# Paged sparse attention of eight sample sequences: from whole-page gathers with a penalty mask to half-page loads and gathers of selected rows

## The chip, the cores and the metric

One core of a Trainium2 chip runs the whole program. The metric is the device time of one execution in microseconds; lower is better. The engines are TensorE (PE, with its weight loads as PEld), VectorE (DVE), ScalarE (ACT), GpSimd (POOL) and SyncE (SP), and 16 DMA engines move data.

## The reference, cut to what matters

The program is one step of a two-layer decoder trunk for a prompt of 512 tokens and for eight sample sequences of one token each. The part that changes is the attention of the sample tokens, once per layer. Each sequence has 4096 past tokens in a paged cache: 32 pages of 128 tokens, four vectors a token (k_cmp, v_cmp, k_sel, v_sel), for 2 groups of 64 numbers. One token is 2 KB, and its first 1 KB is k_cmp and v_cmp.

```python
ck = compress_blocks(k_cmp, ...)      # blocks of 32 tokens, stride 16: 255 rows
cv = compress_blocks(v_cmp, ...)
p_c = masked_softmax(q @ ck * scale + head_bias(rel_bias, dist_c), dist_c >= 0)
o_c = p_c @ cv
p_s = sum over the 4 heads of a group of p_c @ overlap       # a score for each 64-token block
score = where(forced, SEL_FORCE, p_s)                        # first block and the last two are forced
_, idx = top_k(score, 16)                                    # for each sequence and group
o_s = softmax(q @ k_sel[idx] * scale + bias) @ v_sel[idx]
o_w = softmax(q @ k_win * scale + bias) @ v_win              # 512 window tokens and the new one
o = g0 * o_c + g1 * o_s + g2 * o_w
```

## The kernel before, in words

The program is a row of stages, each a block at whose end all engines meet. In each layer the sample attention is one such stage, between the prompt attention and the stage that computes the channel gates (L1695 on). Nothing of the other stages runs beside it, except that SP has loaded the first weights of the next stage ahead. The loop over tiles: a sequence is 8 tiles of 512 tokens. `gather` (L1271 to L1277) copies a column of row numbers into `cell` and issues one indirect DMA on POOL: each of 128 partitions gets 4 whole tokens, 8 KB, 1 MB in all. So all four vectors of all 4096 tokens come in.

For each tile TensorE does this in `turn` and `use`: 8 transposes of k_cmp and v_cmp (L1321), 4 of k_sel (L1326), 4 matmuls with the first compression weights `w1` (L1337), and 4 matmuls of k_sel with the queries `q_blk`, 8 columns each (L1345). DVE lays k_cmp and v_cmp apart (L1497) and copies v_cmp transposes out of PSUM (L1510), ACT those of k_cmp (L1444) and of k_sel (L1448), POOL keeps v_sel (L1285).

The rest of a sequence is `chain`, cut into 13 slots that are put between the tiles of the next sequence by `in_turn`. It has keys in partitions and the 8 heads in columns: second compression matmul, compressed scores, softmax (a maximum over partitions takes a transpose, a reduction and a matmul with `ones`), block scores, top 16 by max and match_replace, a penalty of -1e30 spread to all unselected keys by a small matmul with `rt`, softmax of all 4096 selected-branch scores and the window's, and at slot 11 the value matmuls: 32 over `v_sel` (L1421), 4 over the window (L1424) and a few small ones. For the last sequence the chain runs with nothing beside it.

The setup stage (from time 0) makes the tables: `key_bias` by 40 small matmuls (L695), row numbers from 16 small page-table DMAs on POOL (L628), the input transposes (L716) and the prompt's bias table by a DRAM round trip and 8 `flip` matmuls (L724).

Of the kernel before, what the change touches and what calls it, by code (L numbers as in the profile page):

```python
# [57 lines left out]
BLK = 38  # L58
NEWS, WIN0, NEWW = 32, 33, 37
# [16 lines left out]
def shape_constants():  # L76
# [5 lines left out]
    dist = np.zeros((BLK, P), np.int64)  # L82
    for b in range(32):
        dist[b] = PAST - (STRIDE * (P * (b // 16) + p) + b % 16)
    for t in range(4):
        dist[WIN0 + t] = WINDOW - 4 * p - t
    cmp_dist = np.stack([PAST - (STRIDE * (P * t + p) + CMPB - 1) for t in range(2)])
    keys = onehot(np.concatenate([dist, cmp_dist]))
# [4 lines left out]
    rt = (s[:, None] == n // 4).astype(np.float32)  # L93
    new = np.where(np.arange(NB)[:, None] == np.arange(NB), 0.0, NEG).astype(np.float32)
    kmask = np.zeros((P, 40), np.float32)
    kmask[0, WIN0] = NEG
    kmask[P - 1, 39] = NEG
    chunk = (p % 8).astype(np.float32).reshape(P, 1)
    return {"line": line, "keys": keys.reshape(NBUCK, 40 * P), "ov": ov.reshape(2, P, SELB + 1).transpose(1, 0, 2).copy(),
            "rt": rt, "new": new, "chunk": chunk, "kmask": kmask, "ident": np.eye(P, dtype=np.float32),  # L100
            "flip": np.ascontiguousarray(np.eye(P, dtype=np.float32)[::-1])}
# [19 lines left out]
def build(nc, A, O):  # L121
# [26 lines left out]
    used = {}  # L148

    def sb(scope, name, shape, dt=F32):  # L150

        used[name] = used.get(name, 0) + 1
        if used[name] > 1:
            name = f"{name}_{used[name]}"
        return scope.enter_context(nc.sbuf_tensor(name, shape, dt))

    with stack:
# [12 lines left out]
        rt = sb(stack, "rt", [SELB + 1, 2 * P])  # L170
        key_bias = sb(stack, "key_bias", [P, 40, N_HEADS])
        new_bias = sb(stack, "new_bias", [NB, NB, N_HEADS])
        gather_rows = sb(stack, "gather_rows", [P, NB * 8], U32)
# [366 lines left out]
        cvs = at("cvs", [P, 2, P], F32, offset=w_hi_at + KC * P * 4)  # L540
# [3 lines left out]
        def layer_buffers(L):  # L544
# [4 lines left out]
            for where, name, shape in (("b4", "oac", [P, 6, TOK]), ("b4", "u_c", [P, 2, CC - 1 + TOK]), ("b4", "us_c", [P, 2, CC, NB]),  # L549
                                       ("b3", "w1", [P, 2, 8, P]), ("b3", "w2", [P, 2, P]), ("b3", "b2row", [P, P]), ("b3", "cbias", [P, 2]),  # L550
                                       ("b3", "gateT", [NG_W, TOK]), ("b3", "k_new", [P, 2, NB]), ("b3", "nat_new", [NB, KV_W]),
                                       ("b3", "q_blk", [P, NB, N_HEADS]), ("b2", "z", [P, 20, TOK])):
                S[name] = sb(S[where], f"{name}{L}", shape)
# [8 lines left out]
        with phase_semaphores(), ExitStack() as scope:  # L562
# [6 lines left out]
            keys = sb(scope, "keys", [NBUCK, 40 * P])  # L569
# [176 lines left out]
        for L in range(DEPTH):  # L746
          with phase_semaphores():
# [442 lines left out]
            with phase_semaphores(), ExitStack() as scope:  # L1190
# [62 lines left out]
                def restart_chain(e):  # L1253
                    if e is nc.vector:
                        dve_chain.restart(e)
# [977 lines left out]
```

## Time and profile before

| | |
|---|---|
| Median of 3 runs | 3768.5 us (3766.31 to 3784.81) |
| The profiled execution | 3775.46 us, its span 3773.6 us |
| PE, PEld, DVE, ACT, POOL busy | 89%, 84%, 39%, 25%, 9% |
| Mean granted TensorE clock | 0.856 of 2.4 GHz |
| Moved by DMA | 347.87 MB, mean 92 GB/s |

The span runs from the first to the last instruction; the time of an execution adds 1.9 us around it. Busy shares are averages over stages with different limits. Matmuls in plain f32 appear as two records each and transposes as one, so a count of 64 records at L1421 is 32 matmuls.

### The profile page before, as it was taken

How to read it: one execution, taken by the hardware profiler on the slowest of the kernel's cores; microseconds unless marked ns; L12 is line 12 of the kernel's file. 1: busy time of each engine (PE TensorE's matmuls, PEld its weight loads, DVE VectorE, ACT ScalarE, POOL GpSimd, SP SyncE). 2: the span in 40 equal slices, each digit the busy share in tenths (PEclk: the TensorE clock that was granted, in tenths of full speed). 3: DMA queues.
4: the chain of work that ended last, by engine and by line, in shares of the span. 5: the costliest groups of instructions: out<-in, count | busy, mean ns of one | idle time of the engine just before them, and what ended most of it. 6: DMA issues, size and time to landing. Idle time of an engine off the chain costs nothing. (4 is left out here: it accounts for less than half of the span.)

```text
span 3773.6 us, 57697 instructions
## 1 busy us (share of the span) xinstructions
PE 3364.6 (89%) x22978; PEld 3161.3 (84%) x22978; DVE 1478.1 (39%) x3319; ACT 953.1 (25%) x1827; POOL 351.9 (9%) x470
## 2 busy tenths in 40 slices
PE   5979799898899878999999797989879996899998
PEld 4966688888799868999989566888879996889997
DVE  2235533333646322433231554333427533143322
ACT  0223322221123312222222333221212332132221
POOL 1000122221000100000010002222200000010000
PEclk8977888887799866999989679888969997689998
DMA  5320244342233311233232204443413323023331
GB/s 142 90 81 15 79 164 162 134 150 73 68 85 95 102 60 40 77 92 88 87 80 57 79 12 170 145 154 130 162 28 88 89 82 123 10 65 95 90 89 58
DMA packets 353413, 347.87 MB, mean 92 GB/s; under 512 B 36001, under 2 KB 323110, under 8 KB 336238
## 3 DMA queue, kind: packets, MB, share of 16 engines
q1 hardware_dynamic: 334238, 210.34, 18.8%
q0 software_dynamic: 18944, 134.24, 10.3%
q8 instruction: 170, 2.79, 0.3%
q14 instruction: 61, 0.50, 0.0%
HBM read 333.85 MB, written 19.55 MB: 94 GB/s over the span
## 5 line engine op out<-in xcount | busy, mean ns | idle before, releaser
L313 PE MATMUL pg<-act_hi,w_lo 128*128 128x260 f32 x3072 | 633.9, 288 | 42.7 <-PEq L140 12.6
L285 DVE TENSOR_TENSOR w_lo<-w_raw,w_hi 128x1024 fp32r<-128x1024 f32 x296 | 370.5, 1252 | 712.7 <-ACT w_hi L278 711.7
L313 PE MATMUL pg<-act_hi,w_hi 128*128 128x260 f32 x3072 | 628.0, 287 | 0.0
L313 PE MATMUL pg<-act_lo,w_hi 128*128 128x260 f32 x3072 | 627.4, 286 | 0.0
L313 PEld LDWEIGHTS pg<-act_hi,w_lo 128*128 128x128 f32 x3072 | 484.4, 193 | 47.6 <-issue 32.7
L313 PEld LDWEIGHTS pg<-act_hi,w_hi 128*128 128x128 f32 x3072 | 482.9, 192 | 0.0
L313 PEld LDWEIGHTS pg<-act_lo,w_hi 128*128 128x128 f32 x3072 | 482.8, 192 | 0.0
L278 ACT CAST w_hi<-w_raw 128x1024 fp32r<-128x1024 f32 x296 | 308.5, 1042 | 281.0 <-PE pg L313 141.7
L1448 ACT COPY w_raw<-pg 128x512 f32<-128x512 f32 x144 | 84.6, 587 | 442.1 <-PE pn L1345 439.8
L1421 PE MATMUL pn<-pr,v_sel 128*128 128x8 f32 x1024 | 184.6, 324 | 0.0
L1421 PEld LDWEIGHTS pn<-pr,v_sel 128*128 128x128 f32 x1024 | 183.6, 284 | 0.0
L1321 PE MATMUL pg<-ident,apart 128*128 128x128 f32 x1024 | 161.0, 308 | 14.0 <-DVE apart L1497 14.0
L352 POOL TENSOR_TENSOR norm_r<-norm_ms,minus_half 128x5 f32<-128x5 f32 x12 | 14.1, 1173 | 1609.5 <-DVE norm_ms L348 1609.5
L1321 PEld LDWEIGHTS pg<-ident,apart 128*128 128x128 f32 x1024 | 133.4, 163 | 18.1 <-issue 14.9
L1274 POOL COPY cell<-gather_rows 128x1 uint32 (+1 forms) x128 | 28.4, 222 | 1252.1 <-POOLq L140 691.5
L313 PE MATMUL pg<-hid_hi,w_lo 128*128 128x260 f32 x704 | 142.9, 284 | 0.0
L313 PE MATMUL pg<-hid_hi,w_hi 128*128 128x260 f32 x704 | 141.5, 282 | 0.0
L313 PE MATMUL pg<-hid_lo,w_hi 128*128 128x260 f32 x704 | 141.4, 282 | 0.0
L1345 PEld LDWEIGHTS pn<-q_blk,w_raw 128*128 128x128 f32 x1024 | 134.4, 192 | 6.7
L1276 POOL DMA_INDIRECT cache<-in_cache_kv,cell x128 | 129.9, 1015 | 71.3 <-POOL cell L1274 69.0
L1337 PE MATMUL pg<-xkv,w 128*128 128x256 f32 x512 | 132.3, 404 | 0.0
L1337 PE MATMUL pg<-w_raw,w 128*128 128x256 f32 x512 | 128.7, 396 | 0.9 <-issue 0.2
(407 smaller groups left out, 5504.3 us busy)
## 6 DMA issues: line engine op xcount, KB each, us to landing
w_raw<-in_w_ffn_in SPq DMA_DIRECT2D x88, 512.0 KB, 3.8
w_raw<-in_w_in SPq DMA_DIRECT2D x80, 512.0 KB, 3.8
cmem<-in_cache_mem SPq DMA_DIRECT2D x16, 1024.0 KB, 13.4
w_raw<-in_w_ffn_out SPq DMA_DIRECT2D x32, 512.0 KB, 4.1
win<-in_cache_win SPq DMA_DIRECT2D x16, 512.0 KB, 3.5
w_raw<-in_w_o SPq DMA_DIRECT2D x16, 512.0 KB, 4.2
w_raw<-in_w_xkv SPq DMA_DIRECT2D x16, 512.0 KB, 4.2
out_win_sample<-in_cache_win SPq DMA_DIRECT2D x2, 4088.0 KB
```

Source lines behind the costliest of these rows:

```text
L278: e.copy(w_hi[:, v % 2, :], w_raw[:, v % RING, :]).then_inc(whi_ready, 1)
L285: e.tensor_tensor(w_lo[:, v % 2, :], w_raw[:, v % RING, :], w_hi[:, v % 2, :].bitcast(F32), ALU.subtract).then_inc(w_ready, 1)
L313: mm = e.matmul(pg[:, ts, h, 0:wd], w[:, v % 2, wk], x[:, k0 + k, at:at + wd], start=first and k == 0 and n == 0, stop=last and k == kn - ...
L352: e.tensor_tensor(self.r[:], self.ms[:], minus_half[:, 0:5], ALU.pow).then_inc(rstd_ready, 1)
L1274: e.tensor_copy(cell[:, k % 4:k % 4 + 1], gather_rows[:, bass.ds(b * TILES + k, 1)]).then_inc(cell_set, 1)
L1276: e.indirect_dma_start(out=cache[:, k % 4, :], out_offset=None, in_=rows_dram, in_offset=bass.IndirectOffsetOnAxis(ap=cell[:, k % 4:k % 4 ...
L1321: mm = e.transpose(pg[:, 0, kv, at:at + P], apart[:, k % 2, 2 * kv + g, 2 * pair:2 * pair + 2, :].rearrange("p t d -> p (t d)"), ident[:])
L1337: e.matmul(pg[:, 1, 1, kv * 256:(kv + 1) * 256], w1[:, kv, 2 * (k % 4) + pair, :], xkv[k % 2][:, kv, pair * 256:(pair + 1) * 256], start=k ...
L1345: mm = e.matmul(pn[:, 0, (4 * k + t) * 8:(4 * k + t + 1) * 8], k_sel[:, t * P:(t + 1) * P], q_of(b), start=True, stop=True)
L1421: e.matmul(pn[:, 1, 8:16], v_sel[:, par, t, :], pr[:, t, :], start=t == 0, stop=False)
L1448: e.copy(k_sel[:], pg[:, 1, 0, :]).then_inc(ks_ready, 1)
```

## The change

The sample attention stage is rewritten; the setup makes other tables for it.

- **Half pages.** SP loads for each page only the k_cmp and v_cmp half: 128 tokens of 1 KB, into 8 partitions of `ring`. The page number is read from SBUF into a register (`value_load`) before each of these DMAs. 16 pages make a group of 2 MB; there are 16 groups a layer, so 256 loads and 256 DMAs. `ring` holds two groups.
- **First phase.** POOL lays each half group apart (32 copies of 128x2048). PE makes 136 steps: 128 of 4 transposes and, two steps later, 2 matmuls with `w1`; then 8 for the windows, of 4 transposes and one matmul against the queries. Between them stand the second compression and the compressed scores of each sequence.
- **One chain for all sequences.** The queries sit in `qpad`, 64 columns of which 8 belong to a sequence, so that scores of all eight gather in one PSUM tile with 64 rows (8 sequences by 8 heads) and keys in columns. Softmax is along a row: a maximum from one `tensor_tensor_reduce`, an exponential that also sums. Block lists come from `max` and `max_index`; 13 picked blocks and the forced ones become row numbers `gidx`.
- **Second phase.** POOL issues 16 indirect DMAs for a sequence (8 parts by 2 groups), each of 128 rows of 1 KB (k_sel and v_sel), 128 a layer, all after `gidx` is there. `sel` holds four sequences. PE then transposes the keys, scores them, and after the softmax of a pair of sequences (`q`) multiplies the values.
- Loops over sequences are written out; before they were loops with registers.
- In the setup, 40 small matmuls and the 16 page-table DMAs are gone; two matmuls of 64 rows make `rowbias`, two DMAs on SP bring the page table.

```diff
--- before.py
+++ after.py
@@ setup: tables
-                    for a in range(16):
-                        e.dma_start(pages[8 * a:8 * a + 8, :, :],
-                                    A["page_table"].rearrange("b (t a) -> a b t", a=16)[a:a + 1].broadcast_to([8, NB, 2]), allow_slow_non_contiguous=True
-                                    ).then_inc(ldp, 16)
-                    e.wait_ge(ldp, 256)
+                    for g in range(2):
+                        e.dma_start(pages[g * NB:(g + 1) * NB, :], A["page_table"]).then_inc(ld, 16)
...
+                    for h in range(2):
+                        mm = e.matmul(pg[0:64, 0, h, 0:512 if h == 0 else RB_END - 512], rel8[:].rearrange("p b h -> p (b h)"),
+                                      rows_oh[:, h * 512:512 if h == 0 else RB_END], start=True, stop=True)
@@ sample attention: SP
+                        for n in range(NT):
+                            if n >= 2:
+                                e.wait_ge(laid, 2 * n - 2)
+                            for a in range(16):
+                                page = e.value_load(page_row[0:1, 16 * n + a:16 * n + a + 1])
+                                e.dma_start(ring[8 * a:8 * a + 8, n % 2, :, :],
+                                            A["cache_kv"][L:L + 1, bass.ds(page, 1), :, 0:2].rearrange("l o (c q) k g d -> (l o c) q (k g d)", q=16)
+                                            ).then_inc(got[n % 2], 16)
@@ POOL
+                        for j in range(2 * NT):
+                            n, kv = j // 2, j % 2
+                            if kv == 0:
+                                e.wait_ge(got[n % 2], 256 * (n // 2 + 1))
+                            if j >= 2:
+                                e.wait_ge(turned, 4 * (j - 1))
+                            e.tensor_copy(apart[:, kv].rearrange("p g t d -> p t g d"),
+                                          ring[:, n % 2, :, kv * P:(kv + 1) * P].rearrange("p t (g d) -> p t g d", g=2)).then_inc(laid, 1)
+                        e.wait_ge(gidx_s, 1)
+                        for b in range(NB):
+                            if b == 1:
+                                e.wait_ge(sc_s, NB)
+                            elif 2 <= b < 4:
+                                e.wait_ge(ocw_s, 1)
+                            elif b >= 4:
+                                e.wait_ge(q_pv, (b - 4) // 2 + 1)
+                            for t in range(8):
+                                for g in range(2):
+                                    e.indirect_dma_start(out=sel[:, place[b % 4], t, g, :], out_offset=None, in_=rows_kv,
+                                                         in_offset=bass.IndirectOffsetOnAxis(ap=gidx[:, t, g * NB + b:g * NB + b + 1], axis=0)
+                                                         ).then_inc(sel_in[b], 16)
@@ PE
+                        for m in range(WSTEPS + 4):
+                            if m < WSTEPS:
+                                turn(m)
+                            if 2 <= m < WSTEPS + 2:
+                                use(m - 2)
+                            if (b := at_step(m, 23)) is not None:
+                                compressed(b)
+                            if (b := at_step(m, 27)) is not None:
+                                score_c(b)
...
+                        for b in range(NB):
+                            for hh in range(2):
+                                ktile(b, hh)
+                                kscore(b, hh)
+                            if b % 2:
+                                pturn(b // 2)
+                                values(b // 2)
@@ DVE
+                        link(e.max(top[:, 0:8], score[:]))
+                        link(e.max_index(idx[:, 0:8], top[:, 0:8], score[:]))
+                        link(e.match_replace(score[:], top[:, 0:8], score[:], -1.0))
+                        link(e.max(top[:, 8:16], score[:]))
+                        link(e.max_index(idx[:, 8:16], top[:, 8:16], score[:]))
```

The first place is SP, at the start of the sample attention of the first layer. Before, it issues two window loads and then a loop (L1265) of two more a trip, each with its address computed in a register (ISA) and each a 128x1024 DMA:

```order
L1262 DMA win<-in_cache_win 128x1024 x2
L1265 UNCONDITIONAL_BRANCH
L1265 ISA
L1262 ISA
L1262 DMA win<-in_cache_win 128x1024
L1262 ISA
L1262 DMA win<-in_cache_win 128x1024
L1265 REGISTER_ALU
L1265 COMPARE_AND_BRANCH
```

Now the same place has the page table's load and then three rows for each page, the load of a register, an address computation and a DMA of 8 partitions:

```order
L1267 DMA page_row<-in_page_table 1x256
L1273 TENSOR_LOAD page_row [waits pages_in]
L1274 ISA
L1274 DMA ring_3887<-in_cache_kv 8x16x256
L1273 TENSOR_LOAD page_row
L1274 ISA
L1274 DMA ring_3887<-in_cache_kv 8x16x256
```

The pair of rows repeats 256 times a layer; SP had 272 rows in the whole program and has 1800.

The second place is POOL in the same stage. Before, a gather of 8 KB rows stands between copies, and each waits for its tile buffer:

```order
L1285 COPY v_sel<-cache 128x512 [waits got0]
L1274 COPY cell<-gather_rows 128x1 [waits v_kept,tr_s]
L1276 DMA cache<-in_cache_kv,cell 128x2048 [waits cell_set]
L1285 COPY v_sel<-cache 128x512 [waits got1]
L1274 COPY cell<-gather_rows 128x1 [waits v_kept,tr_s]
L1276 DMA cache<-in_cache_kv,cell 128x2048 [waits cell_set]
```

Now POOL's 32 copies come first (the last two are shown), and all gathers follow them, with a wait at the head of each sequence's 16:

```order
L1290 COPY apart_3889<-ring_3887 128x16x2x64 [waits turned,got1]
L1290 COPY apart_3889<-ring_3887 128x16x2x64 [waits turned]
L1302 DMA sel<-in_cache_kv,gidx 128x256 [waits gidx_s]
L1302 DMA sel<-in_cache_kv,gidx 128x256 x15
L1302 DMA sel<-in_cache_kv,gidx 128x256 [waits sc_s]
L1302 DMA sel<-in_cache_kv,gidx 128x256 x15
L1302 DMA sel<-in_cache_kv,gidx 128x256 [waits ocw_s]
L1302 DMA sel<-in_cache_kv,gidx 128x256 x15
```

The gathers moved from beside the tiles to behind all of them. The third place is PE. Before, one tile of 512 tokens is this:

```order
L1321 MATMUL pg<-ident,apart 128x128 [waits xk_ready,staged]
L1321 MATMUL pg<-ident,apart 128x128 x3
L1321 MATMUL pg<-ident,apart 128x128 [waits xv_ready]
L1321 MATMUL pg<-ident,apart 128x128 x3
L1326 MATMUL pg<-ident,cache 128x128 [waits ks_ready]
L1326 MATMUL pg<-ident,cache 128x128 x3
L1337 MATMUL pg<-w_raw,w 128x256 [waits xk_ready]
L1337 MATMUL pg<-w_raw,w 128x256
L1337 MATMUL pg<-w_raw,w 128x256 [waits xv_ready]
L1337 MATMUL pg<-w_raw,w 128x256
L1345 MATMUL pn<-q_blk,w_raw 128x8 [waits ks_ready]
L1345 MATMUL pn<-q_blk,w_raw 128x8 x3
```

Now 512 tokens are two steps, of these rows, and the second compression (L1349, L1351) stands between steps once in 16:

```order
L1318 MATMUL pg<-ident,apart_3889 128x128 [waits laid,ev0]
L1318 MATMUL pg<-ident,apart_3889 128x128 x3
L1334 MATMUL pg<-w_raw,w 128x256 [waits ev0]
L1334 MATMUL pg<-w_raw,w 128x256
L1318 MATMUL pg<-ident,apart_3889 128x128 [waits ev1]
L1318 MATMUL pg<-ident,apart_3889 128x128 x3
L1334 MATMUL pg<-w_raw,w 128x256 [waits ev1]
L1334 MATMUL pg<-w_raw,w 128x256
```

The transposes and score matmuls of k_sel left the tile.

## Rows read from the trace of the kernel before

**Rows 1.** The page: the span and the engines' busy time and shares.

```profile
span 3773.6 us, 57697 instructions
PE 3364.6 (89%) x22978; PEld 3161.3 (84%) x22978; DVE 1478.1 (39%) x3319; ACT 953.1 (25%) x1827; POOL 351.9 (9%) x470
```

**Rows 2.** Windows: both attention stages, then parts of the first; busy us, PEclk, DMA share, GB/s.

```profile
450.00:976.00 526.00, 461.43 (x2794) 428.10 (x2794) 188.37 (x549) 104.10 (x200) 122.67 (x192) 0.81 0.40 136
2298.00:2813.00 515.00, 449.65 (x2794) 417.83 (x2794) 188.20 (x549) 104.13 (x200) 121.51 (x192) 0.83 0.40 139
...
466.00:490.00 24.00, 23.88 (x170) 22.13 (x170) 9.08 (x13) 7.29 (x14) 12.39 (x19) 1.00 0.88 299
...
540.00:546.00 6.00, 6.00 (x28) 5.90 (x28) 0.27 (x2) 0.00 (x0) 0.00 (x0) 0.50 0.00 0
```

**Rows 3.** Timeline, start and us: first and last instructions of the two stages.

```profile
450.24 0.82 SPq L1262 DMA_DIRECT2D win<-in_cache_win  x2
...
974.83 0.35 DVE L1603 COPY oac<-o 64x4 f32<-64x4 f32 x2
...
2298.27 0.19 POOL L1274 COPY cell<-gather_rows 128x1 uint32<-128x1 uint32 x1 [347.62 <-POOLq L140]
...
2811.70 0.35 DVE L1603 COPY oac<-o 64x4 f32<-64x4 f32 x2
```

**Rows 4.** Timeline of PE in one tile, and the value matmuls of two sequences.

```profile
467.07 1.07 PE L1321 MATMUL pg<-ident,apart 128*128 128x128 f32 x8
468.44 1.89 PE L1337 MATMUL pg<-xkv,w 128*128 128x256 f32 x8
470.17 0.95 PE L1345 MATMUL pn<-q_blk,w_raw 128*128 128x8 f32 x8
...
530.58 12.16 PE L1421 MATMUL pn<-pr,v_sel 128*128 128x8 f32 x64
...
957.64 13.80 PE L1421 MATMUL pn<-pr,v_sel 128*128 128x8 f32 x64
```

**Rows 5.** SP and POOL: durations ns min/median/max of DMA issues and register work; landing.

```profile
L1262 SPq DMA_DIRECT2D win<-in_cache_win x16: 332/336/427, 450.2 to 2699.4; - x16
L1262 SPq FUSED_REGOPS  x12: 43/46/66, 545.7 to 2699.3; - x12
...
L1276 POOL DMA_INDIRECT cache<-in_cache_kv,cell x128: 958/961/1536, 451.1 to 2730.7; - x128
...
L1285 POOL COPY v_sel<-cache x128: 610/627/1132, 458.9 to 2736.2; 128x512 f32<-128x512 f32 x128
...
w_raw<-in_w_c_out SPq DMA_DIRECT2D x16, 128.0 KB, 2.4
```

**Rows 6.** DMA queues: packets, MB, share of the 16 engines over the span.

```profile
q1 hardware_dynamic: 334238, 210.34, 18.8%
q0 software_dynamic: 18944, 134.24, 10.3%
```

**Rows 7.** Timeline of the setup: PE, SP, and the first weight conversion of the next stage.

```profile
24.10 17.23 PE L695 MATMUL pg<-rel,keys 32*128 32x8 f32 x80
...
33.97 0.37 SPq L618 DMA_DIRECT2D toep_up<-line_scratch  x1
...
42.95 5.33 PE L716 MATMUL pa<-ident,x_nat 128*128 128x128 f32 x24
...
53.54 7.61 PE L724 MATMUL pg<-toep_up,flip 128*128 128x512 f32 x16
...
73.99 1.04 ACT L278 CAST w_hi<-w_raw 128x1024 fp32r<-128x1024 f32 x1 [55.16 <-PEq L140]
```

**Rows 8.** DMA issues: KB, and median us to landing of the bias line's load.

```profile
toep_up<-line_scratch SPq DMA_DIRECT2D x1, 2048.0 KB, 7.8
```

**Rows 9.** Timeline of the prompt attention: DVE and ACT on rows of 512.

```profile
2268.29 0.69 DVE L1094 CUSTOM_DVE_ANT_0 s_lg<-pg,toep_h 128x512 f32<-128x512 f32 x1
...
2269.34 0.72 ACT L1160 ACTIVATE s_lg<-s_lg,nmx 128x512 f32<-128x512 f32 x1
```

More of the change, by code:

```diff
@@ L80, in shape_constants @@
     line = onehot(np.maximum(SEQ - 1 - m, 0))
[L82 to L88, printed above, removed]
+    slot = np.arange(SELB)
+    w = np.arange(WINDOW)
+    far = onehot(np.full(SELB, PAST))
+    rows = np.concatenate([
+        onehot(PAST - (STRIDE * np.arange(2 * P) + CMPB - 1)), onehot(WINDOW - (4 * (w % P) + w // P)), onehot(np.zeros(1, np.int64)),
+        np.zeros((NBUCK, SELB), np.float32), onehot(SELB - slot) - far, onehot(np.zeros(1, np.int64)) - far[:, 0:1],
+        onehot(2 * SELB - slot) - far], axis=1)
     n = np.arange(2 * P)
@@ L1467, in _ @@
-                        in_turn(e, tiles, chain)
+                        for m in range(WSTEPS + 4):
+                            if m < WSTEPS and m % 2 == 0:
+                                e.wait_ge(turned, m + 1)
+                                if m >= 4:
+                                    e.wait_ge(used, m - 3)
+                                e.copy(stag[m % 4], pg[:, 0, 0, :]).then_inc(ev[0], 1)
+                            for t in range(2):
+                                if (b := at_step(m, 9 + 8 * t)) is not None:
+                                    keep_half(e, 2 * b + t, c_act, 1)
+                            if (b := at_step(m, 20)) is not None:
+                                e.wait_ge(pre_s, b + 1)
+                                e.activation(second[:, :, 0:2 * P], first[:], ACT.Tanh, scale=0.5).then_inc(th_s, 1)
+                            if (b := at_step(m, 25)) is not None:
+                                e.wait_ge(cmp_s, b + 1)
+                                if b >= 2:
+                                    e.wait_ge(sc_s, b - 1)
+                                e.activation(ck[:, b % 2, :], pn[:, 0, 0:256], ACT.Identity, bias=vecs[:, V_B2:V_B2 + 1]).then_inc(ck_s, 1)
@@ L1605, in _ @@
[L1605 to L1609 removed]
+                            if (b := at_step(m, 25)) is not None:
+                                e.wait_ge(cmp_s, b + 1)
+                                e.tensor_tensor(cv[:, b], pn[:, 1, 0:256].rearrange("p (t x) -> p t x", t=2),
+                                                b2row[:].rearrange("p (o x) -> p o x", o=1).broadcast_to([P, 2, P]), ALU.add).then_inc(cv_s, 1)
```

798 lines of the change are left out of this document (393 added, 405 removed).

## The prediction

> **What bounds the kernel now.** I read the page first [rows 1]. PE is busy 89% of the span, which says little about one stage, so I went on to the windows [rows 2]. The sample attention takes 450.24 to 975.18 in the first layer, 524.9 us, and 2298.27 to 2812.05 in the second, 513.8 us [rows 3]: together 1038.7 us, 28% of the span. In it PE is busy 461 of 526 us at a granted clock of 0.81, while DVE has 188, ACT 104 and POOL 123, and DMA is at 40% [rows 2]. So PE bounds the stage, and the reader should see that its clock is not one value: 1.00 among the tiles (466 to 490) and 0.50 in the value matmuls (540 to 546). The timeline gives the prices at full clock: 1.07 us for the 8 transposes of k_cmp and v_cmp in a tile, 1.89 us for its 4 matmuls with `w1`, 0.95 us for its 4 matmuls of k_sel with the queries [rows 4]. The 32 value matmuls of a sequence cost 12.16 us, or 0.38 us each, at the low clock [rows 4]. Beside the last sequence nothing runs, and its value matmuls take 13.80 us with everyone waiting [rows 4].
>
> **What leaves PE.** A sequence loses 32 transposes of k_sel, the 32 small score matmuls over all keys and most of the value matmuls. What a tile keeps, 1.07 + 1.89 us, is now two steps of 1.48 us. I add 1.6 us a sequence for the second compression and its scores (four matmuls, priced from the 0.47 us of one with 256 columns, 1.89 / 4). A window step has 4 transposes (0.54), one matmul of 512 columns (7.61 / 8 = 0.95, [rows 7]) and a small one: 1.7 us. PE's work in the first phase is 8 x (16 x 1.48 + 1.6) + 8 x 1.7 = 216 us, or 12.6 us for a group of 16 pages. That alone would end the stage early. The question is who feeds it.
>
> **First phase: SP.** SP now does three things for each of 256 pages: a register load, an address computation, a DMA. Two of them have rows: an address computation 0.046 us, a DMA with a computed address 0.336 us [rows 5]. The register load has none. Bounds: not below the 0.05 us of a register operation, not above the 2.4 us that the quickest DMA in the page takes from issue to landing [rows 5], since that contains a read of memory and much besides. I am nearer to neither row, so I reason from the second: it holds descriptor making, a read, a write and a semaphore, and the register load is the read alone, a quarter to a third. I take 0.7 us. A page then costs s = 0.70 + 0.05 + 0.34 = 1.09 us, a group 17.4 us against PE's 12.6. **SP becomes the bound of the phase.** Length: page table there 2.9, 256 x 1.09 = 279, last landing 2.4, POOL's copy 2.5 (4 x 0.627, [rows 5]), the last 8 steps 11.8, windows 13.6, last compression 1.6: **314 us**. POOL's 32 copies (5 us a group) and the copies of DVE and ACT lie beside that. The ring of two groups does not bind: a slot comes free about when SP has issued the group before.
>
> The Trainium skill, "DMA: Bandwidth & Descriptors", Latency and other measured facts, gives about 600 ns as the floor of a tensor_load. By it the phase would be 288 us and the kernel 3633 us; no row here shows it.
>
> **The transfers.** The queues give 34 ns for a packet on one engine at a mean of 629 bytes (0.188 x 16 x 3773.6 / 334238) and 328 ns at 7086 bytes [rows 6]; a straight line puts a row of 1 KB at 52 ns. A group has 2048 rows: 6.7 us over 16 engines, hidden under 17.4. A DMA into 8 partitions may not use all of them; over 8 engines it is 13.3 us, still hidden, but it would bind if the register load cost under 0.44 us. The same page of the Trainium skill, How many engines (k), says that the largest number up to 16 that divides the slowest dimension of both sides is used, here 8. By it the floor of my range for a free register load is 3552 us, by 16 engines 3518.
>
> **Between the phases.** Until the first gather may go there is one serial chain with nothing beside it: about 25 small DVE operations at 0.2 to 0.25 us, three over 806 numbers (1.35 ns each from 0.69 us for 512, [rows 9]) 3.3 us, two exponentials and row reads 1.5 us, 16 matmuls that spread the row numbers at 0.38 us, six handovers. Sum **18 us**, no less than 12 and no more than 28.
>
> **Second phase: POOL.** 128 gathers of 128 rows. An indirect issue takes POOL 0.961 us and has 128 rows before as well [rows 5], so 123 us, all after the last score, where before they lay beside PE. Then the last sequence: landing 2.4; transposes, scores, copies 4.6; softmax over 961 numbers 4.7 (1.3 and 1.35 for the two long ones after [rows 9]); turning and keeping 1.8; the 36 value matmuls of a pair at 0.38, 13.7; the last addition 0.6. Together **151 us**. The gathers of the fifth sequence wait until the first pair's values are done: landed at 33 us, done at about 58, and POOL comes there at 61. Slack of 3 us, so no stall in the sum.
>
> **Setup.** The 40 matmuls of L695 hold PE for 17.23 us, and the input transposes and flips follow [rows 7]. With them gone the flips wait for the load of the bias line instead, issued at 33.97 and landed 7.8 us later [rows 7, 8]. They start at 41.8, not 53.54, and each later event, the weight conversion at 73.99 included, moves up by **11.7 us**.
>
> **Sum.** Stage 314 + 18 + 151 = 483 us; 41.9 and 30.8 us less than the two of before, with the setup 84 us less. Against this execution's 3775.46 us that is 3691; the median of the runs shown is 7 us lower, so 3684. With s free the time is 3684 + 512 x (s - 1.09): each 0.1 us of a page's issue is 51 us, and **at s = 1.25, a register load of 0.87 us, the gain is gone**. Half a percent, 19 us, is about what a measurement can tell from no change.
>
> **Rivals.**
> - *The register load costs 0.9 us or more* (slower). Place: SP at L1273. At 1.1 us s is 1.49, each first phase 102 us longer, time 3889. For: the load lies in the path of every page, nothing overlaps it on SP, and no row bounds it well. Against: only my split of the 2.4 us. Chance 0.33. At the far bound of 2.4 us it would be 4555.
> - *SP is fast and PE or the transfers bind.* Register load below 0.6 us; 3518 to 3635, by the work of 216 us or the 8 engines. For: register operations are cheap in all rows. Chance 0.14.
> - *The second phase costs more.* An issue of 1.3 us (the longest row is 1.54) gives 43 us a layer, a missed slack at the fifth and seventh sequence 5 us each. Time 3740 to 3790: no change that can be told. Chance 0.10.
> - *PE's clock stays low.* With gaps of 5 us a group PE might run at 0.50 as in 540 to 546: a step of 2.96, a group of 25 us, time about 3970. Against: at half clock PE would have no gaps, and among dense tiles it is granted 1.00. Chance 0.05.
> - *The forecast*: s from 1.0 to 1.19, 3640 to 3735 us. Chance 0.38.
>
> **Numbers.** Faster 0.38 + 0.14 = 0.52, same 0.10, slower 0.33 + 0.05 = 0.38. The cases have both signs, so the range must reach into them: 3600 to 3980 leaves out a register load under 0.54 us and one above 1.28 us, some 0.2 together.
>
> **What would show it.** The register load's duration on SP; the distance between page DMAs, 1.09 us; POOL's laying copies waiting for DMA and not for PE; first phase of 314 us; 128 gathers back to back at 0.96 us, PE mostly idle under them; L278 first at about 62 us. I am wrong if POOL waits for PE in the first phase, or if SP's row is far from 0.7.

## The result, and the profile after

The changed kernel takes **4105.8 us** (median of 4 runs, 4093.9 to 4115.6) against 3768.3 us before (4 runs): ratio 1.088, 95% interval 1.084 to 1.093. It is slower by 9%; the forecast was 3685 us. The profiled execution took 4115.6 us.

The page of the changed kernel, beside [rows 1]:

```profile
span 4113.8 us, 52582 instructions
PE 3158.6 (77%) x20942; PEld 2874.3 (70%) x20942; DVE 1335.2 (32%) x2724; ACT 896.1 (22%) x1725; POOL 464.0 (11%) x390
```

PE lost 206 us of work, as meant, and the span grew by 340 us: PE now waits. Two views say for what. First the timeline of SP in both layers, and of the last DVE instruction of each stage (start, us, instruction):

```profile
436.56 0.26 SPq L1267 DMA_DIRECT2D page_row<-in_page_table  x1
438.45 450.26 SPq L1274 DMA_DIRECT2D ring<-in_cache_kv  x256
...
2452.03 0.26 SPq L1267 DMA_DIRECT2D page_row<-in_page_table  x1
2453.92 455.72 SPq L1274 DMA_DIRECT2D ring<-in_cache_kv  x256
...
1124.08 0.44 DVE L1658 TENSOR_TENSOR oac<-pa,o_cw 64x32 f32<-64x32 f32 x2 [8.91 <-PE pa L1465]
...
3144.54 0.43 DVE L1658 TENSOR_TENSOR oac<-pa,o_cw 64x32 f32<-64x32 f32 x2 [8.91 <-PE pa L1465]
```

The stages are 436.56 to 1124.52, 688.0 us, and 2452.03 to 3144.97, 692.9 us, where [rows 3] had 524.9 and 513.8: 342 us more, which is the whole loss. Of each, SP spends 450 and 456 us on its 256 pages, register loads and transfers in turn: 1.76 and 1.78 us a page.

Then the lines of SP's instructions (durations in ns, min/median/max), to set beside [rows 5]:

```profile
L1273 SPq TENSOR_LOAD <-page_row x512: 463/816/913, 437.8 to 2907.9; - x171
L1274 SPq FUSED_REGOPS  x512: 37/44/51, 438.3 to 2908.8; - x171
L1274 SPq MOVE ring<-in_cache_kv x512: 29/38/42, 438.4 to 2908.9; - x171
L1274 SPq DMA_DIRECT2D ring<-in_cache_kv x512: 702/711/1946, 438.5 to 2908.9; - x171
...
  POOL apart L1290: 1504.1, 32
```

The register load costs 0.816 us and the issue 0.711 us, twice the 0.336 of the window's load. In the first layer all 256 issues together are only 3 us over 256 times their shortest length, and SP stands still for more than 0.3 us only eight times, 2.9 us in all: nothing but its own instructions holds SP up. The last line says who waits for these transfers: POOL's laying copies, 1504 us in the whole stream of its 32 waits (of which the long idle time before each stage's first is a part). In the timeline of POOL the groups of 16 pages come at this pace:

```profile
471.45 3.72 POOL L1290 COPY apart<-ring 128x2048 f32<-128x2048 f32 x2 [381.60 <-DMA ring<-in_cache_kv]
500.75 3.73 POOL L1290 COPY apart<-ring 128x2048 f32<-128x2048 f32 x2 [25.57 <-DMA ring<-in_cache_kv]
...
893.79 3.73 POOL L1290 COPY apart<-ring 128x2048 f32<-128x2048 f32 x2 [25.33 <-DMA ring<-in_cache_kv]
```

28.2 us a group on average over 15 distances, each copy waiting for DMA. The windows of the first phase, the chain between, the gathers, and the first phase of the second layer (columns as in [rows 2]):

```profile
436.00:905.00 469.00, 213.18 (x1059) 178.94 (x1060) 74.73 (x142) 54.93 (x107) 59.67 (x32) 0.72 0.46 81
925.00:937.00 12.00, 3.87 (x50) 3.12 (x50) 9.03 (x35) 1.69 (x5) 0.00 (x0) 0.58 0.00 1
937.00:1085.00 148.00, 94.70 (x487) 72.12 (x486) 20.96 (x48) 11.06 (x22) 112.26 (x117) 0.53 0.33 102
...
2440.00:2935.00 495.00, 222.89 (x1154) 186.51 (x1154) 82.36 (x164) 60.61 (x122) 59.66 (x32) 0.73 0.48 77
```

PE is busy 213 of 469 us at a granted clock of 0.72: it has the work that was forecast, and waits for more than half of the time. The DMA share of 0.46 is 0.92 of eight engines, so by itself it would fit a bound by the transfers as well; the experiments have to tell the two apart. In the second phase POOL's gathers start 1.25 us apart, not 0.96:

```profile
937.41 1.18 POOL L1302 DMA_INDIRECT sel<-in_cache_kv,gidx  x1 [39.88 <-DVE gidx L1608]
938.89 0.95 POOL L1302 DMA_INDIRECT sel<-in_cache_kv,gidx  x1 [0.30 <-issue]
940.14 0.95 POOL L1302 DMA_INDIRECT sel<-in_cache_kv,gidx  x1 [0.30 <-issue]
```

Each carries 0.30 us in which POOL waited for nothing that the profile shows.

### The profile page after: what moved, and what is told of

Its sections match the earlier page's. It is cut to its first block and busy times, and to the rows that moved or that the text cites. A ratio compares the mean times of both kernels' runs of the same rounds, so it can differ in the third digit from the quotient of the medians.

```text
span 4113.8 us, 52582 instructions
## 1 busy us (share of the span) xinstructions
PE 3158.6 (77%) x20942; PEld 2874.3 (70%) x20942; DVE 1335.2 (32%) x2724; ACT 896.1 (22%) x1725; POOL 464.0 (11%) x390
## 5 line engine op out<-in xcount | busy, mean ns | idle before, releaser
L309 PE MATMUL pg<-act_hi,w_lo 128*128 128x260 f32 x3072 | 633.0, 288 | 42.2 <-PEq L135 11.9
L1318 PE MATMUL pg<-ident,apart 128*128 128x128 f32 x1024 | 186.6, 315 | 519.6 <-POOL apart L1290 519.6
L1318 PEld LDWEIGHTS pg<-ident,apart 128*128 128x128 f32 x1024 | 149.7, 165 | 562.1 <-issue 465.6
L1550 DVE COPY w_raw<-pg 128x512 f32<-128x512 f32 x136 | 94.0, 691 | 789.2 <-PE pg L1318 776.3
L1334 PE MATMUL pg<-w_raw,w 128*128 128x256 f32 x1024 | 305.2, 427 | 0.0
L1290 POOL COPY apart<-ring 128x2048 f32<-128x2048 f32 x64 | 119.3, 1893 | 1504.1 <-DMA ring<-in_cache_kv 1504.1
L1302 POOL DMA_INDIRECT sel<-in_cache_kv,gidx x256 | 246.8, 964 | 156.6 <-DVE gidx L1608 79.2
L1334 PEld LDWEIGHTS pg<-w_raw,w 128*128 128x128 f32 x1024 | 202.9, 220 | 19.6
L338 PE MATMUL pa<-ones,sq_hi 128*128 128x1 f32 x640 | 106.8, 298 | 24.2 <-ACT sq_hi L331 24.2
L338 PEld LDWEIGHTS pa<-ones,sq_hi 128*128 128x128 f32 x640 | 107.1, 262 | 25.7 <-ACT sq_hi L331 25.7
```

What stands on the lines that cost most here:

```text
L309: mm = e.matmul(pg[:, ts, h, 0:wd], w[:, v % 2, wk], x[:, k0 + k, at:at + wd], start=first and k == 0 and n == 0, stop=last and k == kn - ...
L338: mm = e.matmul(self.sums[:, tt:tt + 1], self.sq[:, n % SLOTS, at:at + P], ones[:, 0:1], start=c == 0 and tt == 0, stop=c == KC - 1, skip_ ...
L1290: e.tensor_copy(apart[:, kv].rearrange("p g t d -> p t g d"), ring[:, n % 2, :, kv * P:(kv + 1) * P].rearrange("p t (g d) -> p t g d", g=2 ...
L1302: e.indirect_dma_start(out=sel[:, place[b % 4], t, g, :], out_offset=None, in_=rows_kv, in_offset=bass.IndirectOffsetOnAxis(ap=gidx[:, t, ...
L1318: mm = e.transpose(pg[:, 0, m % 2, (2 * i + g) * P:(2 * i + g + 1) * P], cut, ident[:])
L1334: mm = e.matmul(pg[:, 1, n % 2, kv * 256:(kv + 1) * 256], w1[:, kv, 2 * ip + i, :], stag[m % 4][:, i * 256:(i + 1) * 256], start=m % 8 == ...
```

## Experiments

Theory A: SP's own instructions (load and issue) set the first phase. Theory B: the transfers themselves do, since a page goes to 8 partitions only. A time is one run unless a count stands with it; the kernel before gave 3770 to 3779 us beside them.

**static_pages**: no register load; each page transfer has a constant address, so the address work is gone too, and the compressed branch works over other pages than the table names.

```diff
-page = e.value_load(page_row[0:1, 16 * n + a:16 * n + a + 1])
+page = 16 * n + a
```

> SP reads no page number: each page DMA has a constant address (page 16n+a), so the compressed branch works on other pages than the table names. Bytes, rows and the 8-partition form of each DMA stay. Theory A (SP's issue bounds the first phase): a page costs the DMA issue alone, 0.71 us at most, a group of 16 about 12 us; PE (12.6 us and more) or the transfers bind next, a group 14 us or less, the kernel 3620 to 3700 us. Theory B (the transfers bind, because a DMA into 8 partitions runs on half of the engines: share 0.46 of 16 in the changed kernel, 0.92 of 8): a group stays near 26 us, the kernel at 4030 to 4100 us.

3752.4 us, 353 us less than the changed kernel, but 52 us over the range of theory A. So what a page costs on SP is most of the loss. But the pace is not even. Windows, and SP's issues, early and late in the phase:

```profile
476.00:516.00 40.00, 16.61 (x72) 14.10 (x73) 3.46 (x5) 2.93 (x5) 5.40 (x3) 0.63 0.57 60
...
676.00:716.00 40.00, 40.00 (x245) 34.45 (x244) 19.22 (x30) 13.19 (x27) 11.69 (x7) 1.00 0.55 183
...
L1274 SPq DMA_DIRECT2D ring<-in_cache_kv x20: 1998/2062/2769, 474.4 to 515.8; - x20
...
L1274 SPq DMA_DIRECT2D ring<-in_cache_kv x56: 667/667/752, 675.7 to 715.4; - x56
```

Early, 60 GB/s arrive while the DMA engines are busy at 0.57, and a group takes 35 us, longer than with the loads; late, 183 GB/s at the same share, PE busy all the time at clock 1.00, a group in 11.5 us. The issue tells where SP is held: 2.06 us early, 0.667 late. With the loads gone something in the transfers holds the first half of the phase: A and B both have a part. In the second layer the same 256 transfers took 226 us where they took 310 in the first.

**loads_by_8**: the loads of eight pages together, then their eight transfers.

```diff
+read = [e.value_load(page_row[0:1, 16 * n + a:16 * n + a + 1]) for a in range(8 * h, 8 * h + 8)]
+for a, page in zip(range(8 * h, 8 * h + 8), read):
+    e.dma_start(...)
```

> The same 256 register loads a layer, but eight in a row ahead of eight DMAs instead of one before each. If a load is a round trip that later loads can overlap, eight cost about 1.5 us and not 6.5, a page 0.95 us, a group 15 us, the kernel near 3690 us. If SP waits for each load before it goes on, nothing moves: group 28 us, the kernel within 10 us of 4106. Theory B also says no change, but then with page DMAs issued in bursts and SP waiting for a free half of the ring.

3905.4 us, 200 us less, but far from the 3690 that I expected. Of the 512 loads the median falls to 0.268 us. The lines of SP:

```profile
L1273 SPq TENSOR_LOAD <-page_row x512: 260/268/929, 437.3 to 2685.8; - x171
L1275 SPq DMA_DIRECT2D ring<-in_cache_kv x512: 671/676/2616, 440.0 to 2692.4; - x171
```

So a load behind another load is 0.27 us; the 0.82 is what a load costs behind one of these transfers (the first of each eight still costs about that). SP's 256 pages took 341.7 us, 1.33 a page, where the two medians make 0.94. My sum had left out the address work and the distances between instructions, 0.22 us a page here; the first loads of each eight add 0.06, and issues of up to 2.6 us another 0.11, so that SP is now held back a little itself. The groups take 17 to 29 us, early and late alike.

**two_queues**: SP makes 10 transfers of a group, ACT's queue 6.

> SP issues 10 of the 16 pages of a group and ScalarE's queue the other 6, each with its own register load. Theory A: a group takes 10 x 1.76 = 17.6 us, 10.6 us less than now, 170 us a layer, the kernel near 3770 us; ACT gets 10.6 us of issue a group beside 6 us of copies, so somewhat more, up to 3830. Theory B: the same bytes on the same 8 engines, a group of 26 us, the kernel above 4030 us.

3803.9 us, 302 us less, within the range of theory A: a group takes 15 to 20 us in the first layer, 17.2 on average, and SP's 160 pages take 282.0 us, again 1.76 each. An issue costs ACT 1.182 us (median of 192) where it costs SP 0.712. Two queues side by side make the pace 1.6 times that of one with the same transfers, at 115 to 137 GB/s and a share of 0.54 to 0.56, which a bound by the transfers alone would not allow.

**whole_tokens**: no page loads on SP; POOL gathers whole tokens, 128 rows of 8 KB an instruction (twice the bytes), by row numbers made once in the setup, as before; all else as changed.

```diff
+e.indirect_dma_start(out=ring[:, j % SLOTQ].rearrange("p t x -> p (t x)"), out_offset=None, in_=rows_4,
+                     in_offset=bass.IndirectOffsetOnAxis(ap=gather_rows[:, j:j + 1], axis=0)).then_inc(got[j % SLOTQ], 16)
```

> First phase fed as in the kernel before: POOL gathers whole tokens, 1 MB at a time (64 gathers a layer, rows of 8 KB, all 16 engines), into a ring of six, and lays k_cmp and v_cmp apart by 4 tokens; k and v steps alternate. No register load, no page DMA on SP. The one chain and the second phase stay as in the changed kernel. Twice the bytes of the half pages in this phase. Theory A and the engine rule both say that PE binds then: 216 us of steps and some 15 us of start, a first phase of 230 to 260 us against 488, and the kernel at 3570 to 3640 us, below both. Rival: 4 MB a group at about 400 GB/s is 10.5 us, close to PE's 12.6, so with waits a group of 16 us and 3680 us.

**3536.3 us** (median of 4, 3529.5 to 3543.8), ratio to the kernel before 0.937, interval 0.934 to 0.940: it beats both kernels, and lies 34 us under the range that I gave. A window of its first phase:

```profile
520.00:560.00 40.00, 40.00 (x245) 34.53 (x244) 18.37 (x28) 12.60 (x25) 28.96 (x29) 1.00 1.00 399
```

PE is busy 40 of 40 us at clock 1.00, and 399 GB/s arrive where page transfers passed 193 in no window that I read. The first gather leaves at 441.3 and the first of the second phase at 656.4. So PE's part of the first phase works at least as well as forecast, and the way in which the halves are loaded is what undid the change; the second phase is as long as in the changed kernel (656.4 to 842.6, 186 us, for 151 forecast).

**wide16**: the same 128 rows to 16 partitions x 8 tokens. They land in other places, so the compressed branch works over other keys.

```diff
-e.dma_start(ring[8 * a:8 * a + 8, n % 2, :, :], ...rearrange("l o (c q) k g d -> (l o c) q (k g d)", q=16)
+e.dma_start(ring[16 * (a % 8):16 * (a % 8) + 16, n % 2, 8 * (a // 8):8 * (a // 8) + 8, :], ...q=8)
```

> Edit: each page's transfer goes to 16 partitions x 8 tokens in place of 8 partitions x 16 tokens; the same 128 rows of 1 KB, the same register load. The rows land in other places, so the compressed scores and the blocks chosen are of other keys; nothing else changes. SP's own issue is the bound (the theory): register load 0.82 us and transfer issue 0.71 us stay, a group of 16 pages stays at 28.2 us, time 4080 to 4130 us. The eight engines are the bound (rival): an instruction that writes 8 partitions keeps half the engines busy and its issue is held back; with 16 partitions the issue falls to about 0.34 us and a group to about 22 us, time near 3910 us. If a slimmer instruction alone is what costs, the issue gets dearer with 16 partitions, and the time goes above 4150 us.

3740.6 us, 365 us less than the changed kernel, by this alone: a miss for the theory as I had put it, since both instructions got cheaper, and 169 us under the rival's 3910 too. Its lines and its timeline:

```profile
L1273 SPq TENSOR_LOAD <-page_row x512: 262/266/481, 435.4 to 2541.4; - x171
L1274 SPq DMA_DIRECT2D ring<-in_cache_kv x512: 563/564/1511, 436.1 to 2541.8; - x171
...
436.10 272.59 SPq L1274 DMA_DIRECT2D ring<-in_cache_kv  x256
```

1.065 us a page, steady from the first group to the last (17.0 us): what I had forecast for a page (1.09), by other terms. With it the prediction's own formula gives 3671 us; the second phase, 36 us a layer longer than forecast, makes 3743 of it, beside the 3741 measured. The Trainium skill, "DMA: Bandwidth & Descriptors", How many engines (k), says that a transfer uses the largest number of engines up to 16 that divides the slowest dimension of both sides, so 8 before and 16 here. The traces agree: between 480 and 640 us the changed kernel has 736 packets of 4 bytes beside 92 page transfers, 8 for each, and wide16 has 2409 beside 151, 16 for each. The share fits roughly: long_rows, below, stays at 0.50, other 8-partition runs go up to 0.58 while page transfers alone run, and wide16_loads8 reaches 0.98 in one window; what makes it more than 0.50 was not followed up. But wide16 moves its bytes no faster than SP issues them, so its gain is the 0.55 us off the load and the 0.15 off the issue, not the eight engines more.

**doubled_loads**: every page number read twice.

> Edit: every page's number is read twice into a register, the second is used; the result is the same. 512 loads more. If what a load costs is its own 0.82 us, each one whole: 512 x 0.82 = 420 us more, 4525 us. If two loads in a row overlap (as the eight in a row did, 0.27 us each, by their rows), the second adds 0.27 us: 140 us more, 4245 us. If the transfers bind the phase and not SP, nearly nothing is added, under 4150 us.

4097.0 us. It decides nothing, and none of its three cases was tried: its trace holds 512 register loads, not 1024, so the load whose value nobody used never reached the chip. It is a second run of the changed kernel.

**long_rows**: 64 rows of 2 KB into the same 8 partitions, whole tokens of half a page. **interleaved**: partition c takes tokens c, c + 8, ... in place of 16 neighbours. In both the compressed branch works over other data.

```diff
-...rearrange("l o (c q) k g d -> (l o c) q (k g d)", q=16)
+...rearrange("l o (q c) k g d -> (l o c) q (k g d)", q=16)    (interleaved)
```

> Edit: a page's transfer takes 64 rows of 2 KB (whole tokens, the first 8 of each 16) in place of 128 rows of 1 KB, into the same 8 partitions; bytes, register load and everything behind are the same, the compressed branch works over other numbers. In wide16 the transfer's issue fell from 0.71 to 0.56 us and the register load behind it from 0.82 to 0.27 us. If that comes from 8 rows a partition in place of 16 (rows set the price), it falls here too: a page near 1.06 us or below, time 3740 us or less. If it comes from 16 partitions in place of 8 (what an instruction spreads over), load and issue stay at 0.82 and 0.71 us and the time at 4080 to 4130 us.

> Edit: partition c of a page takes tokens c, c + 8, c + 16, ... in place of 16 neighbouring ones, so that what the partitions read at one moment lies 2 KB apart and not 32 KB; same rows, partitions, register load; the compressed branch works over tokens in another order. If SP's two instructions set the page (the theory), nothing changes: groups of 28 us, 4080 to 4130 us. If transfers that meet in memory hold the issue back (rival), packets get shorter, the register load falls below 0.6 us and the time below 3950 us.

long_rows 3782.6, interleaved 3874.7 us. Issues fell to 0.308 and 0.317 us, the load behind them to 0.53. Both expectations had one trait for both prices, and neither holds as written: the partitions were not what made the issue dear. In the early groups (26 and 34 us) both stay behind what SP's prices and distances would give, in the late ones (some 17 us) not.

**static_scattered** and **static_interleaved**: as static_pages, with page numbers that jump (`(16 * n + a) * 149 % 256 + 3`), or with interleaved tokens: does the order of addresses make the early groups slow?

> Edit: as static_pages (constant page numbers, no register load, so the compressed branch works over other pages), but the constant numbers jump through the pool (149 times the index modulo 256, plus 3) where static_pages took neighbours one after another. There the first groups took 30 to 35 us and the later ones 11 to 16 us. If neighbouring pages are what made the first groups slow, every group takes 11 to 17 us here and the time is 3600 to 3680 us. If the form of the transfer (8 partitions) or SP's queue sets it, the groups look as in static_pages and the time is within 30 us of 3752 us.

> Edit: static_pages (constant page numbers, no register load) with the token order of interleaved. In static_pages the first eight groups took 16 to 35 us each at 60 to 100 GB/s and the last ones 11.5 us at 184 GB/s, with the engines' share at 0.55 to 0.57 in both, so each packet took three times as long at first. If that comes from reads 32 KB apart meeting in memory until the engines have drifted apart, all groups take 11 to 14 us here and the time is 3580 to 3660 us. If it is not the address order, the groups look as before and the time is within 30 us of 3752 us.

3783.1 and 3755.4 us, 31 and 3 us above static_pages. Early groups are 30.6 and 32 us where static_pages had 35, late ones 11.5 in all three. Neither order is the cause by itself; the slow start of transfers to 8 partitions **stays open**.

**wide16_loads8**: both edits.

> Edit: wide16 with the register loads of eight pages made together ahead of their eight transfers. In wide16 a page takes 1.06 us: load 0.27, issue 0.56, address and small ones 0.07, and 0.16 between them. If SP's sum sets it and each load costs the same 0.27 us behind a transfer or behind a load, nothing is won: 3720 to 3750 us. If a switch from transfer to load costs the 0.16 us too, a page falls to 0.9 us, a group to 14.5 us, and the time by 2 x 16 x 2.5 = 80 us to 3660 us, near the 12.6 us of PE's work. If the transfers are then the bound, groups stay at 17 us.

3757.2 us, no less than wide16, as the first case of the expectation had it (7 us over its range). One of its windows, then SP's whole work on the 256 pages and, from just ahead of that window, eight loads and their eight transfers:

```profile
516.00:556.00 40.00, 29.85 (x157) 24.57 (x156) 10.56 (x18) 8.52 (x17) 7.46 (x4) 0.87 0.87 122
...
438.61 275.47 SPq L1276 DMA_DIRECT2D ring<-in_cache_kv  x256
...
L1274 SPq TENSOR_LOAD <-page_row x8: 265/268/276, 506.5 to 508.6; - x8
...
L1276 SPq DMA_DIRECT2D ring<-in_cache_kv x8: 563/564/572, 509.0 to 514.2; - x8
```

The share is 0.87 where wide16 had 0.65 in the same stretch, at 122 GB/s in place of 125, so the share looks like a bound by the transfers. SP's starts say otherwise. Eight loads start 0.29 us apart and eight transfers 0.75 us apart, 1.04 us a page or 16.6 us a group, without an idle stretch on SP or a long issue; the groups take 17.4. What the expectation hoped for, a saving of 0.16 us at each switch, isn't there, because every instruction on SP has its distance to the next, loads among loads too. So SP still sets nearly the whole pace in wide16 and here, with an issue of 0.56 us as its largest part, and no run shows what the transfers to 16 partitions could do under a faster issue, beyond the two groups of each form in the next run.

**forms**: two groups each in eight forms, one trace.

> Edit: two groups of 16 pages each in eight forms of the page's transfer, one after the other in both layers; the compressed branch works over other data in most. Groups 0, 1: as in the changed kernel (8 partitions, one run of 128 rows 2 KB apart). 2, 3: 8 partitions, tokens interleaved. 4, 5: 16 partitions, neighbouring tokens. 6, 7: 16 partitions, interleaved. 8, 9: 8 partitions, 16 KB in one piece each. 10, 11: 16 partitions, 8 KB in one piece each. 12, 13: as 0, 1 with a constant page number. 14, 15: as 4, 5 with a constant page number. The single runs gave issue and register load as 0.71 and 0.82, 0.32 and 0.53, 0.56 and 0.27, (none), 0.31 and 0.53, (none). If 8 partitions are what makes the load behind a transfer dear, groups 6, 7 and 10, 11 show 0.27 us loads and the 8-partition ones 0.53 us or more; if the run of neighbouring rows is what makes the issue dear, groups 6, 7 have an issue near 0.31 us and so a page under 0.8 us, 12 us a group if the transfers keep up. If both only follow how fast the queues drain, prices in a group here differ from those of the single runs. No time of the whole is told by it; about 3850 us as the mean of the single runs.

The whole took 3779.2 us, 71 us under the mean that I had named. Its use is in the lines of the forms with a register load (issue in ns), and in SP's timeline, where 32 transfers take 55.7, 41.8, 37.2, 25.6, 33.2 and 25.1 us, and 32.2 and 31.4 in the two forms without a load:

```profile
L1283 SPq DMA_DIRECT2D ring<-in_cache_kv x64: 702/711/844, 439.7 to 2345.7; - x64
L1285 SPq DMA_DIRECT2D ring<-in_cache_kv x64: 307/356/1322, 496.4 to 2385.4; - x64
L1287 SPq DMA_DIRECT2D ring<-in_cache_kv x64: 563/564/1190, 539.0 to 2421.8; - x64
L1289 SPq DMA_DIRECT2D ring<-in_cache_kv x64: 316/317/781, 576.7 to 2448.5; - x64
L1291 SPq DMA_DIRECT2D ring<-in_cache_kv x64: 306/311/327, 604.9 to 2482.7; - x64
L1294 SPq DMA_DIRECT2D ring<-in_cache_kv x64: 315/315/1227, 638.9 to 2509.8; - x64
...
439.70 55.73 SPq L1283 DMA_DIRECT2D ring<-in_cache_kv  x32
...
576.67 25.57 SPq L1289 DMA_DIRECT2D ring<-in_cache_kv  x32
```

The register loads between them, by stretch (8 partitions neighbouring, 8 interleaved, 16 neighbouring, 16 interleaved, 8 in one piece, 16 in one piece):

```profile
L1279 SPq TENSOR_LOAD <-page_row x14: 785/840/867, 466.9 to 490.4; - x14
L1279 SPq TENSOR_LOAD <-page_row x20: 523/558/599, 496.8 to 519.5; - x20
L1279 SPq TENSOR_LOAD <-page_row x12: 262/267/273, 562.3 to 574.2; - x12
L1279 SPq TENSOR_LOAD <-page_row x15: 262/267/273, 577.0 to 588.5; - x15
L1279 SPq TENSOR_LOAD <-page_row x13: 502/529/671, 616.9 to 629.7; - x13
L1279 SPq TENSOR_LOAD <-page_row x12: 261/266/270, 650.2 to 659.3; - x12
```

Two traits, two prices. Neighbouring tokens taken by half, rows 2 KB apart in one run, make the **issue** 0.56 to 0.71 us; interleaved rows or whole pieces, 0.31 to 0.32. Eight partitions make the **load behind** 0.53 us, sixteen 0.27; and with both traits it is 0.82 to 0.84. The changed kernel has the worst form of the six, 1.74 us a page, and 16 interleaved partitions the second best, 0.80. The single runs agree to 0.03 us, but for the interleaved issue at 8 partitions, whose median of 0.36 here hides two kinds: 0.31 in its first group, 0.75 in its second, where the transfers hold it back. So theory A holds for the changed kernel, with prices that the form of the transfer sets. Theory B is the bound behind it in the runs with the cheaper 8-partition forms (static_pages and its two variants, interleaved, in part loads_by_8 and long_rows), where issues grow past their shortest length or SP waits; in wide16 and wide16_loads8 SP is still the bound. Why a form has its price no run shows. A kernel with 16 partitions and the compressed branch intact (its matmuls would have to take half blocks) was not tried.

**one_group**: half of the second phase's gathers; key group 1 reads group 0's rows, so the other engines keep their work.

```diff
-for g in range(2):
+for g in range(1):
```

> Edit: in the second phase only the gathers of key group 0 are made (8 a sequence in place of 16), and group 1 reads group 0's rows, so that half of the selected keys and values are wrong; PE, DVE and ACT do the same work. POOL's issue is the bound (the theory): 64 gathers fewer a layer at 1.25 us, 80 us a layer, less what then comes to wait for PE. The last sequence's chain (26 us) and the pairs' work stay; PE has about 12 us a pair of value matmuls and some 5 us a sequence before them, so that it could become the bound at 90 to 100 us. Time 3945 to 4000 us. Rival, transfers or the pairs' chain bind: the second phase stays at 187 us within 20 us, time 4065 to 4106 us.

4010.6 us, 95 us less. The second phase falls from 187.1 us (937.41 to 1124.52) to 144.3 (933.78 to 1078.04). POOL's timeline shows the next bound:

```profile
975.01 0.95 POOL L1302 DMA_INDIRECT sel<-in_cache_kv,gidx  x1 [0.30 <-issue]
984.87 0.94 POOL L1302 DMA_INDIRECT sel<-in_cache_kv,gidx  x1 [8.92 <-PE pa L1465]
```

POOL's issue is the bound of the second phase, but only for 43 us of the 80 that it would give up: PE's value matmuls are next, POOL waits for them for 8.9 us here and 11.9 us one pair later. The time is 11 us above the range that I gave.

## Why the prediction was wrong

The structure of the sum stood; one term of it broke the result, and a second was too small.

- **First phase: SP** (314 us, "a page then costs s = 1.09"). This is the step that failed. That SP becomes the bound was right, and so was the price of a page's time: 512 x (1.76 - 1.09) = 343 us, and the two first phases are about that much longer. The time of a page was wrong, 1.76 us for 1.09. The register load is 0.816 us for 0.70, and the DMA issue 0.711 us for 0.336; 0.23 us a page are the address work and the move (0.08) and the distances between instructions, for 0.05. The issue was the larger miss, 0.375 of 0.67 us, against 0.116 and 0.18 for the others, and I had given it no bound: the price was taken from a load of 128 partitions in whole pieces, and a transfer of another shape was costed as if it were the same. The kernel before could have warned me, since transfers of the very 128 KB of a page stand in its trace at nearly twice that price:

```profile
L269 SPq DMA_DIRECT2D w_raw<-in_w_nsa_out x32: 607/617/717, 1107.4 to 2992.7; - x32
```

The load I bounded, but as a thing by itself. Behind another load, or a transfer to 16 partitions, it is 0.27 us (loads_by_8, wide16, forms); it costs 0.82 because of the transfer ahead of it. With only the load at its measured price s would have been 1.21 and the forecast 3743 us; with only the issue, 1.46 and 3874.
- Measured first phase: 488.4 us (436.56 to 925.0): 1.9 for the page table, 450.3 for the pages, 36 for the rest, where 2.9, 279 and 31.9 were forecast.
- **The transfers** ("hidden under 17.4"). A group over 8 engines was put at 13.3 us, from 52 ns for a row. At 183 GB/s the late groups of static_pages bear that out: 16 engines x 0.55 x 40 us over 7150 rows of 1 KB are 49 ns. The early ones need 156 ns a row (0.57 x 16 x 40 us over 2344 rows), and in the changed kernel it is about 93 ns (0.46 x 16 x 469 us over 37100 rows). So the row was no constant. At s = 1.76 the transfers stay hidden all the same, since SP's issues show no holdup; they bind in the early groups of the 8-partition runs once SP is relieved. That no page-transfer version fell under 3740 us has three causes: this slow start, what SP still costs with 16 partitions, and the second phase.
- **Between the phases**: 18 us forecast, 12.4 measured (925.0 to 937.41), at the lower bound.
- **Second phase: POOL** (151 us; measured 187.1). Its own mis-sized term: 128 gathers at 0.961. They take 1.25 us each, 160 us, since 0.30 us lie ahead of each. In the kernel before, a small copy stands ahead of each gather, and its profile puts 0.27 us of the idle time before a gather down to a wait for that copy; I took the duration alone:

```profile
485.15 0.96 POOL L1276 DMA_INDIRECT cache<-in_cache_kv,cell  x1 [0.27 <-POOL cell L1274]
```

The rival of a dearer second phase had this nearly right (an issue of 1.3 us, 43 us a layer). The tail was 25.0 us for 28. The slack at the fifth sequence was no stall, as said.
- **Setup**: the first weight conversion is at 57.42, 16.6 us earlier than in [rows 7], and the stage starts 13.7 us earlier than in [rows 3], for 11.7.
- **PE's work**: 216 us forecast for the first phase; a group at full clock takes 11.5 us for 12.6 (static_pages, late, where SP's issues, 0.72 us from start to start, give the same 11.5). The clock, 0.72 in the phase, was no bound: POOL waited for DMA, not for PE.

Put together: 3691 us forecast for the execution, + 205.0 and 209.9 us for the two stages, - 2.0 for the setup, + 11.7 for the stretches behind the stages (1323.1 to 1327.5 and 961.6 to 968.8 us; not followed up) are 4115.6, the measured time. The rival of a dear register load had the sign, the place and the price for each 0.1 us right, and the mechanism only in part: it named the load, not the transfer that makes it dear and its own issue. The outcome lay beyond its 3889 and beyond the range, since both of SP's terms rose together and the range was made by letting only the load move.

## What to carry to other kernels

A DMA's issue has no one price: before 256 of them go on a queue, find a row of the same shape (partitions, length and distance of the rows), and without one let the issue vary as widely as the instruction that is plainly unknown. Count a serial loop by the distance between starts, not by the sum of durations; the idle time ahead of each instruction is part of its price even where the profile puts a waiting releaser beside it. A high share of busy DMA engines is no proof that the transfers bind; look first whether the queue that issues them ever stands still. Half the bytes as 256 page transfers from SP came in more slowly than all of them as 64 gathers of 8 KB rows from POOL: here reading twice as much and using half was 570 us faster. The two differ in the issuing engine, the kind of DMA, the number of issues and the row length at once, and no run separates these.

## What the runs showed of the hardware

- A register load on SP takes 0.27 us behind another load or behind a transfer to 16 partitions (loads_by_8, wide16, forms), 0.53 us behind one to 8, and 0.82 us behind one to 8 that takes the halves of neighbouring tokens, 2 KB apart in one run. The Trainium skill, "DMA: Bandwidth & Descriptors", Latency and other measured facts, puts a floor of about 600 ns under it; the 0.27 us here are below that.
- On SP the issue of 128 rows of 1 KB costs 0.71, 0.56 or 0.32 us by their order and the partitions (forms), and its instructions lie some 0.04 us apart, so that a page in wide16_loads8 takes 1.04 us for 0.90 us of durations; ACT's queue asks 1.18 us for what SP issues in 0.71.
- Indirect DMAs back to back on POOL start 1.25 us apart with 0.95 us of duration each.
- The share of busy DMA engines does not measure the rate: at 0.55 to 0.57 the rate was 60 GB/s early and 183 late in one kernel. Why rows to 8 partitions arrive so slowly in the first 80 to 200 us of the first layer's phase isn't known; it shows with rows of 2 KB too (long_rows, 69 to 107 GB/s in its first 120 us) and not with 16 partitions at SP's pace; the order of pages and that of tokens are ruled out as its only cause.
